# Variances of the heads: two rounded matmuls of high and low parts in place of one fp32 matmul

## The reference, cut to what matters

```python
def head_norm(y, w, center):
    b, t, h, d = y.shape
    if center:
        y = y - jnp.mean(y, axis=-1, keepdims=True)
    y = y * lax.rsqrt(jnp.mean(y * y, axis=-1, keepdims=True) + EPS)
    return y.reshape(b, t, h * d) * w.astype(jnp.float32)
...
y_b = head_norm(retention(rq, rk, rv), ret_gn_w, center=True) * jax.nn.silu(rg)
y_c = head_norm(gated_linear_attention(gq, gk, gv, log_a), gla_gn_w, center=False) * jax.nn.silu(gr)
```

## Time and profile before

| | us |
|---|---|
| median of 3 runs (lowest, highest) | 2785.6 (2785.32, 2787.62) |
| the profiled execution's own time | 2787.1 |
| its span in the trace | 2785.3 |
| TensorE busy | 2761.2 (99%) |
| VectorE busy | 1506.4 (54%) |
| ScalarE busy | 1046.5 (38%) |
| GpSimd busy | 57.0 (2%) |
| TensorE's share of the chain that ended last | 94% |

### The profile page before, as it was taken

How to read it: one execution, slowest core, us unless ns; L and a number is a source line. 1 busy time by engine, 2 the same in 40 slices (tenths; PEclk the granted TensorE clock), 3 DMA queues, 4 the chain that set the end, 5 groups by cost and what they waited for, 6 DMA issues and landing times.

```text
span 2785.3 us, 36204 instructions
## 1 busy us (share of the span) xinstructions
PE 2761.2 (99%) x13664; PEld 2295.6 (82%) x13664; DVE 1506.4 (54%) x2130; ACT 1046.5 (38%) x1450; POOL 57.0 (2%) x59
## 2 busy tenths in 40 slices
PE   9999999999999999999999999999999999999998
PEld 7887888888888888788888888888888877888887
DVE  6944555654434784555565443554434688554433
ACT  5335533432223433643342232432223457432221
POOL 0030000000000003000000000000000000000000
PEclk9999999999999999999999999999999999999999
DMA  4242333233332223133323333233333320233332
GB/s 143 84 121 59 91 100 105 76 106 98 95 99 86 84 88 117 54 102 94 110 79 106 92 98 98 75 110 97 92 98 101 110 92 2 76 106 98 96 98 78
DMA packets 80088, 258.55 MB, mean 93 GB/s; under 512 B 9936, under 2 KB 12368, under 8 KB 79472
## 3 DMA queue, kind: packets, MB, share of 16 engines
q1 hardware_dynamic: 74160, 248.57, 29.6%
q10 hardware_dynamic: 5824, 8.55, 1.2%
HBM read 247.38 MB, written 2.10 MB: 90 GB/s over the span
## 4 chain that ended last, share of the span: by engine, by line
PE 94%; DVE 4%; ACT 1%; issue 1%; DMA 0%; ACTq 0%; SPq 0%; DVEq 0%
PE bank L428 29%; PE bank L430 29%; PE bank L429 29%; PE bank L1067 1%; PE bank L1283 1%; PE bank L1303 1%; PE bank L1274 1%; DVE w_lo L571 1%; PE bank L1083 1%; PE bank L1114 1%; PE bank L1122 0%; ACT w_hi L567 0%; DVE x L730 0%; DVE u_lo L667 0%; DMA raw<-in_weights 0%
## 5 line engine op out<-in xcount | busy, mean ns | idle before, releaser
L428 PE MATMUL bank<-u_hi,w_hi 128*128 128x512 f32 (+1 forms) x2632 | 1007.1, 383 | 6.2 <-DVE scratch L836 2.8
L430 PE MATMUL bank<-u_hi,w_lo 128*128 128x512 f32 (+1 forms) x2632 | 991.3, 377 | 0.0
L429 PE MATMUL bank<-u_lo,w_hi 128*128 128x512 f32 (+1 forms) x2632 | 991.2, 377 | 0.0
L571 DVE TENSOR_TENSOR w_lo<-raw,w_hi 128x1024 fp32r<-128x1024 f32 x490 | 603.9, 1233 | 621.8 <-ACT w_hi L567 610.3
L567 ACT ACTIVATE w_hi<-raw 128x1024 fp32r<-128x1024 f32 x490 | 514.8, 1051 | 351.6 <-PE bank L430 324.6
L428 PEld LDWEIGHTS bank<-u_hi,w_hi 128*128 128x128 f32 x2632 | 495.7, 188 | 107.4 <-issue 8.6
L429 PEld LDWEIGHTS bank<-u_lo,w_hi 128*128 128x128 f32 x2632 | 495.8, 188 | 93.6 <-issue 5.5
L430 PEld LDWEIGHTS bank<-u_hi,w_lo 128*128 128x128 f32 x2632 | 495.5, 188 | 90.9
L428 PE MATMUL bank<-hid_hi,w_hi 128*128 128x512 f32 (+1 forms) x792 | 290.3, 367 | 0.0
L430 PE MATMUL bank<-hid_hi,w_lo 128*128 128x512 f32 (+1 forms) x792 | 289.7, 366 | 0.0
L429 PE MATMUL bank<-hid_lo,w_hi 128*128 128x512 f32 (+1 forms) x792 | 289.6, 366 | 0.0
(11 more groups left out here) (261 smaller groups left out, 2594.5 us busy)
## 6 DMA issues: line engine op xcount, KB each, us to landing
raw<-in_weights SPq DMA_DIRECT2D x410, 512.0 KB, 3.5
raw<-in_weights SPq DMA_DIRECT2D x48, 256.0 KB, 2.7
raw<-in_weights SPq DMA_DIRECT2D x32, 384.0 KB, 3.1
rot_s<-rot_in ACTq DMA_DIRECT2D x32, 128.0 KB, 2.3
q_s<-q_in ACTq DMA_DIRECT2D x52, 64.0 KB, 2.6
x<-in_x SPq DMA_DIRECT2D x4, 512.0 KB, 6.4
ret_mask<-in_ret_mask SPq DMA_DIRECT2D x2, 1024.0 KB, 6.2
out<-x SPq DMA_DIRECT2D x16, 128.0 KB, 1.7
```

Of the source, the lines that this page charges most:

```text
L428: nc.tensor.matmul(out, st_hi, mv_hi, start=first, stop=False)
L429: nc.tensor.matmul(out, st_hi, mv_lo, start=False, stop=False)
L430: return nc.tensor.matmul(out, st_lo, mv_hi, start=False, stop=last)
L571: nc.vector.tensor_tensor(w_lo[:, bl.slot(p), :], raw[:, bl.raw(p), :], w_hi[:, bl.slot(p), :].bitcast(F32), ALU.subtract).then_inc(lo_spl ...
```

## The change

`head_copy` on ScalarE makes a third instruction: it waits for its own square and copies it, rounded, to `sq_hi`. With head 0 of each layer it also rounds the matrix of ones to `ones_r` (128x128). VectorE gets `square_low`, which subtracts the rounded square from the square and writes the rest in place over the square (`sq_lo` is the same memory as the two tiles of `sq_h`). `head_var` on TensorE now waits for `square_low` instead of the square, and issues two float32r matmuls into the same bank, with the same weights. `ones_r` and `sq_hi` move the tiles placed after them by 4.5 KB per partition. The order of all else is kept.

```diff
--- before.py
+++ after.py
@@ -222,8 +222,11 @@
         row_sum = place("row_sum", [P, 4])
         row_inv = place("row_inv", [P, 4])
         wait_cell = place("wait_cell", [P, 40])
+        ones_r = place("ones_r", [P, P], F32R)
+        sq_hi = place("sq_hi", [P, 2, T], F32R)
         scratch_at = top[0]
         S = [place(f"scratch{i}", [P, T]) for i in range(5)]
+        sq_lo = place("sq_lo", [P, 2, T], F32R, scratch_at + 2 * 4 * T)
         arena = top[0]
         KB = 1024
         place("arena", [P, 88 * KB // 4])
@@ -369,6 +372,8 @@
         rv_sum = ev("rv_sum", 4)
         rv_cent = ev("rv_cent", 4)
         hn_sq = ev("hn_sq", 8)
+        hn_hi = ev("hn_hi", 8)
+        hn_lo = ev("hn_lo", 8)
         hn_rr = ev("hn_rr", 8)
         hn_y = ev("hn_y", 8)
         silu_g = ev("silu_g", 8)
@@ -1116,10 +1121,11 @@
 
             def head_var(n, li):
 
-                pe.wait_ge(hn_sq.sem, hn_sq.upto(li, n + 1))
+                pe.wait_ge(hn_lo.sem, hn_lo.upto(li, n + 1))
                 use = side(f"var{n}", li)
                 pe.wait_ge(use.drained, use.n + 1)
-                nc.tensor.matmul(use.mem[:, :], ones_c, sq_h[n % 2][:, :], start=True, stop=True).then_inc(use.filled, 1)
+                nc.tensor.matmul(use.mem[:, :], ones_r[:, :], sq_hi[:, n % 2, :], start=True, stop=False)
+                nc.tensor.matmul(use.mem[:, :], ones_r[:, :], sq_lo[:, n % 2, :], start=False, stop=True).then_inc(use.filled, 1)
 
             def layer(li):
                 bl, ou, s = Blocks(li * (N_LAYER // 4)), layer_outs(li), li * 2
@@ -1337,6 +1343,10 @@
                 src = side(f"out{n}", li)
                 act.wait_ge(src.drained, src.n + 2)
                 nc.scalar.activation(sq_h[n % 2][:, :], y, ACT.Square).then_inc(hn_sq.sem, 1)
+                act.wait_ge(hn_sq.sem, hn_sq.upto(li, n + 1))
+                if n == 0:
+                    nc.scalar.activation(ones_r[:, :], ones_c, ACT.Copy)
+                nc.scalar.activation(sq_hi[:, n % 2, :], sq_h[n % 2][:, :], ACT.Copy).then_inc(hn_hi.sem, 1)
 
             def head_rsqrt(n, li):
                 use = side(f"var{n}", li)
@@ -1701,6 +1711,12 @@
                 dve.wait_ge(rot_moved[i % 2], li * 128 + (i // 2 * 32 + 32))
                 nc.vector.tensor_tensor(rot_s[:, i % 2, :], rot_s[:, i % 2, :], ret_sin[:, :], ALU.mult).then_inc(rot_z.sem, 1)
 
+            def square_low(n, li):
+
+                dve.wait_ge(hn_hi.sem, hn_hi.upto(li, n + 1))
+                nc.vector.tensor_tensor(sq_lo[:, n % 2, :], sq_h[n % 2][:, :], sq_hi[:, n % 2, :].bitcast(F32),
+                                        ALU.subtract).then_inc(hn_lo.sem, 1)
+
             def head_norm(n, li):
                 y = (y_c if n < 4 else y_b)[:, n % 4, :]
                 gain = (P_GLAGN if n < 4 else P_RETGN) + n % 4
@@ -1811,6 +1827,8 @@
                         nc.vector.scalar_tensor_tensor(rot_in[:, i % 2, :], use.mem[:, :], P ** -0.5, r[:, :], ALU.mult, ALU.mult).then_inc(use.drained, 1)
                     else:
                         nc.vector.tensor_tensor(rot_in[:, i % 2, :], use.mem[:, :], r[:, :], ALU.mult).then_inc(use.drained, 1)
+                    if 2 <= i <= 5:
+                        square_low(i - 2, li)
                     if i >= 1:
                         rotated(i - 1, li)
                     if 3 <= i <= 6:
@@ -1833,15 +1851,19 @@
                 for h in range(HEADS):
                     split(GR + h)
                     gate_in(h, bl, ou, li)
+                    if h >= 2:
+                        square_low(2 + h, li)
                     ret_decay(h, li)
                     gated(h, li)
                     if h == 3:
                         head_norm(4, li)
                 split(RG)
                 gate_in(4, bl, ou, li)
+                square_low(6, li)
                 head_norm(5, li)
                 gated(4, li)
                 split(RG + 1)
+                square_low(7, li)
                 gate_in(5, bl, ou, li)
                 head_norm(6, li)
                 gated(5, li)
```

## The result

| | median us (lowest, highest, runs) | ratio to before, 95% interval |
|---|---|---|
| before | 2786.64 (2785.07, 2787.62, 11) | |
| changed | 2792.34 (2790.50, 2795.74, 11) | 1.0022 (1.0015 to 1.0030) |

The forecast was 2790.7, with 2788.2 to 2796.5 as its range. The profiled execution took 2792.15 us, its span 2790.3.

The account below looks back on a forecast made before the run. TensorE, busy 99% of the span and 94% of the chain, was taken as the bound. Per layer -3 x 0.40 + 1.33 + 2.44 = +2.57, in all +5.1 on the median 2785.6, gave 2790.7 us, range 2788.2 to 2796.5.

Parts of the forecast that it names:

- The pair saves 0.40: At each variance on TensorE, two float32r matmuls take 0.46 us instead of 0.86, saving 0.40 where nothing waits.
- Heads 0 to 2 and 4 are covered: At these heads the subtraction ends before TensorE needs it, by 0.4 us at heads 0 to 2; each saves 0.40.
- Head 3 stands still 1.6 and leaves 1.33 late: At head 3 TensorE waits some 1.6 us for the subtraction behind an eviction; its projection resumes 1.33 us late, saving included.
- Heads 5, 6 and 7 leave 0.09, 0.26 and 2.44 late: In the stage of the gates, ScalarE's added copies and VectorE's subtractions make TensorE resume these us late, 2.44 holding all.
- the alternative of 4.7 us: If ScalarE's added copies overlap by 93 ns and cost 0.54 us each, the sum is an estimated +4.7 us.
- The milder form: Head 7's wait is only the 1.5 us forced by order, ScalarE making up its delay: 2788.9 us, chance 0.09.
- +2.57 a layer, +5.1 in all, waits above 6 us: Sum of the heads' savings and delays per layer and for two; under 6 us of TensorE waits would refute it.
- the rival by which ScalarE's copies reach TensorE as late weights: Each layer's 8 added copies arrive as late low weights, 5.2 us on top, 2795.9 us; chance 0.06.
- The granted clock still 1.00 behind it: Sign in the changed kernel's trace: the clock stays at full behind TensorE's wait of some 2.5 us at head 7.
- The rival: The clock falls behind head 7's stillness, costing 2.0 to 8.0 us, so 2792.7 to 2798.7 us; chance 0.18.
- Nothing is given back in the gate loop: After the stage of the gates TensorE is fed three blocks ahead, so its delay of 2.44 us stays.
- Cover everywhere: Rival: every subtraction is done before the projection ends, so 6.4 us are saved, 2779.2 us; chance 0.07.

Follow-up runs that it names:

- e3: Changed kernel without the rounding copy and subtraction; both float32r matmuls read one square rounded as made, low part left out: 2780.45 us, ratio 0.9978 to before.
- e11: The changed kernel run again, unaltered, on one chip with the fillers of e12: 2793.04 us, ratio 1.0023 to before.
- e9: Changed kernel with every subtraction at the end of the turn before, ahead of the low weights too: 2780.62 us, ratio 0.9978 to before.
- e10: e9 with GpSimd instead of ScalarE rounding the squares of heads 4 to 7: 2780.44 us, ratio 0.9977 to before.
- e5: Changed kernel with head 3's subtraction alone moved in front of the eviction of its turn: 2790.94 us, ratio 1.0016 to before.
- e4: Changed kernel keeping copy, subtraction and wait, but with the one fp32 variance matmul of before instead of the pair: 2797.31 us, ratio 1.0041 to before.
- e2: Changed kernel with head 7's subtraction alone moved in front of the low weights of its turn: 2786.51 us, ratio 1.0001 to before.
- e8: Changed kernel with head 7's subtraction moved later, behind the eviction and normalisation of head 6: 2797.70 us, ratio 1.0041 to before.
- e1: Changed kernel with subtractions moved early: heads 0 to 3 before their turn's eviction, 4 to 7 to the turn before's end: 2781.44 us, ratio 0.9981 to before.
- e6: Changed kernel with useless matmuls in front of TensorE's wait, 6 at head 3 and 9 at head 7: 2792.26 us, ratio 1.0020 to before.
- e7: e1 with GpSimd instead of ScalarE rounding the squares of heads 4 to 7: 2780.79 us, ratio 0.9980 to before.
- e12: Changed kernel with useless matmuls before TensorE's waits at heads 3, 5, 6 and 7 (6, 2, 1, 10): 2792.89 us, ratio 1.0023 to before.

## Why the prediction was right

The direction, the mechanism and its two places were right; the size was short by 0.6 us of the 5.7 between the medians, and the one step that the traces contradict is that on the clock. The forecast of 2790.7 stood 1.6 us under the measured 2792.3; the other 1.0 is the median of before, 2785.6 in the three runs that it started from and 2786.64 in eleven. That the profiled executions agree with it to 0.1 us (2792.2 forecast, 2792.15 measured) is luck: the changed kernel's trace has a fall of 1.6 us behind head 7 that was not forecast, and lacks the one that before has at 2264.

- **The pair saves 0.40.** Confirmed: 2.40 - 2.01 = 0.39 at head 0, 6.45 for 16 heads in e3. The pair itself took 2.01 - 1.54 = 0.47 there, for 0.46.
- **Heads 0 to 2 and 4 are covered.** Confirmed: no wait there; head 0's cover was 0.44 us, for the 0.4 forecast.
- **Head 3 stands still 1.6 and leaves 1.33 late.** The wait was 1.45. The rotation stage as a whole came to +0.21 and +0.16, where the steps give -3 x 0.40 + 1.33 = +0.13.
- **Heads 5, 6 and 7 leave 0.09, 0.26 and 2.44 late.** The projections resumed at 261.81, 270.42 and 278.97; less what stood in the step's own sums (261.50, 269.99 and 276.34) and the 0.16 carried into the stage, that is +0.15, +0.27 and +2.47. The low weights of head 7's turn started at 276.51, less 0.16 that is 276.35, for the 276.33 forecast. So ScalarE's copy in front of a table load did cost its full 0.65 (0.66 in the rows above), and the alternative of 4.7 us, worked with an overlap of 93 ns, was not borne out.
- **The milder form** falls with it: head 7's wait is 2.3 us and not the 1.5 that the order alone forces.
- **+2.57 a layer, +5.1 in all, waits above 6 us.** Where the clock stayed, a layer cost 0.16 + 2.44 = 2.60, twice that 5.2; the waits were 9.5. So the rival by which ScalarE's copies reach TensorE as late weights, 5.2 us on top, did not come either: there is no room for it in the stages.
- **"The granted clock still 1.00 behind it."** Wrong in part. It fell behind head 7 in one layer of the first profile and both of e11's, at 1.5 to 1.7 us each (4.04 and 4.11, or 3.91, less 2.44), short of the 2.0 that the rival had as its smallest price. In the changed kernel's mean it would carry 6.3 - 5.2 = 1.1 us, an estimate only, since the ratio's interval is 4 us wide; what is shown is the price in a trace that has it. The mean granted clock that is on record for every execution, to three digits, points the same way: 0.9981 over the 22 of this kernel (e11 with them) against 0.9985 over 85 of before, which at half speed while low is an estimated 1.0 us. Of the 22, the six at 0.999 took 2790.5 to 2792.3 us, the four at 0.997 took 2794.6 to 2796.0. The rival stood at 0.18 as a case beside mine; it is one laid over mine, in some executions and layers. The Trainium skill (TensorE: Matmul & The Clock Gate, section What's actually happening) has the clock halve after an idle window. The traces agree that a lone wait of 2.4 us amid dense work can bring this, and show that it need not.
- **Nothing is given back in the gate loop.** Confirmed: the shift at the feed-forward anchor holds all of it, +2.44 in layer 2.
- **Cover everywhere** was not the case here, and is what e9 and e10 make of the code. Its price, 6.4 us, is what they gained (6.1 and 6.4 in the mean).

What stays open: why the same wait of 2.3 to 2.4 us brought a fall in five of six layers of the profiles of the changed kernel, e5 and e11, and none in the sixth, and why e4's wait of 1.95 us did so in one layer of two. In the means, by the estimate of 1.0 to 1.1 us for two layers at 1.6 each, it comes less often than in these traces. The waits of 0.3 to 1.5 us at heads 3, 5 and 6 brought none in any trace of these.

## What to carry to other kernels

A cheaper instruction on the bounding engine is worth its saving only where its inputs come as early as they did: before swapping an operation for one with a preparation step, put the preparation at the end of the turn before, ahead of whatever in its engine's order waits for someone else. On an in-order engine, position decides more than cost: 0.68 us of VectorE work, placed behind one instruction instead of ahead of it, cost 2.65 us a layer (2.44 + 0.21, the changed kernel against e2). Compare two kernels by the start of the same instruction at a few anchors; the same stage came out within 0.1 us here in all traces without a fall, where whole times of one kernel lay 2.1 to 5.3 us apart.

## What the runs showed of the hardware

- A wait inside dense work costs more than its length when the clock falls behind it: 1.5 to 1.7 us behind a wait of 2.4 us (five of six), 1.7 in e4 behind one of 1.95 (one of two), some 2.7 in e8 behind one of 3.6 (two of two).
- A ScalarE copy of 128x512 between its own square, for which it waits, and a table load costs 0.66 us from start to start; with nothing between, such copies stood 0.52 apart.
- The fall of before at 2264 comes and goes between executions of the same code: the changed kernel's profile has 1.00 there, e11's 0.61 somewhat later:

```profile
2272.00:2276.00 4.00, 2.11 (x12) 1.16 (x12) 2.93 (x6) 2.48 (x8) 0.00 (x0) 0.61 0.06 23
```

Its price in the profile of before was 1.9 us by the shift account. The other traces bear it out: behind the second layer's anchor the seven without a fall there (changed, e2, e3, e4, e5, e8, e9) gained 1.5 to 2.0 us on before, the six with one (e1, e6, e7, e10, e11, e12) between a gain of 0.4 and a loss of 0.3. The times of before lie in two clusters, near 2785.3 and 2787.1, which fits: of the 85 executions of before beside the experiments, the 39 with a granted clock of 0.999 took 2785.8 us in the mean, the 46 with 0.998 took 2787.2. An experiment that takes this fall away was not made.
